# Down projection of a decoder layer: two chunk pairs as plain products, weight sums made in small units

## What is computed

```python
u, val = jnp.split(h2 @ p['w_up'], [D_FF], axis=-1)
u, fbuf_new = causal_dwconv(u, fbuf, p['ffconv_w'], p['ffconv_b'])
x = x + g2 * ((jax.nn.silu(u) * val) @ p['w_down'])      # (2048 + 32, 2816) @ (2816, 1024)
...
y_prompt = rms_norm(h_p, final_w)
```

## Time and profile before

| | us |
|---|---|
| median of 3 runs | 2711.03 (2708.97 to 2712.45) |
| profiled execution, device time | 2711.22 |
| its span on the trace | 2709.4 |
| end of the up stage, start of the down stage | 2240.4 |
| last matmul of the 88 steps ends | 2687.3 |
| TensorE busy, share of the span | 2463.4 (91%) |

### The profile page before, as it was taken

The page is one execution under the profiler, slowest core; times in us unless marked ns, Lnnn a source line. Parts: engine busy times, 40 slices in busy tenths (PEclk is TensorE's granted clock), DMA queues, the critical chain, the costliest instruction groups (busy, mean ns, idle before and its releaser), DMA issues. The chain is left out here.

```text
span 2709.4 us, 44409 instructions
## 1 busy us (share of the span) xinstructions
PE 2463.4 (91%) x17038; PEld 1519.8 (56%) x17038; DVE 1884.9 (70%) x3863; ACT 913.0 (34%) x1376; POOL 403.2 (15%) x384
## 2 busy tenths in 40 slices
PE   3899999879889999599969999999999986899997
PEld 1455555567677777455546666666666652344443
DVE  4555556446888887578866777777777779867666
ACT  1433433214444445144422222222222224322222
POOL 0132322300000000012332221222122200000000
PEclk6899999989999999599989999999999997899999
DMA  7434443460242312233312221122212214333323
GB/s 259 153 103 142 162 143 107 148 195 21 86 172 95 124 58 63 88 121 120 120 51 74 74 78 62 62 73 78 74 49 73 79 63 164 117 90 105 105 87 93
DMA packets 197350, 279.80 MB, mean 103 GB/s; under 512 B 19023, under 2 KB 134271, under 8 KB 195059
## 3 DMA queue, kind: packets, MB, share of 16 engines
q1 hardware_dynamic: 196965, 278.18, 31.4%
q10 hardware_dynamic: 270, 0.10, 0.0%
HBM read 202.95 MB, written 75.29 MB: 103 GB/s over the span
## 5 line engine op out<-in xcount | busy, mean ns | idle before, releaser
L2553 PE MATMUL py<-h_parts,w_heads 128*128 128x384 f16 (+1 forms) x792 | 246.0, 311 | 19.1 <-DVE u_p L2710 19.1
L2554 PE MATMUL py<-h_parts,w_heads 128*128 128x384 f16 (+1 forms) x792 | 245.8, 310 | 0.0
L2555 PE MATMUL py<-h_parts,w_heads 128*128 128x384 f16 (+1 forms) x792 | 245.8, 310 | 0.0
L336 PE MATMUL prj<-w_heads,h_parts_t 128*128 128x512 f16 x512 | 196.1, 383 | 12.3 <-PEq L451 6.2
L337 PE MATMUL prj<-w_heads,h_parts_t 128*128 128x512 f16 x512 | 195.8, 382 | 0.0
L338 PE MATMUL prj<-w_heads,h_parts_t 128*128 128x512 f16 x512 | 195.7, 382 | 0.0
L336 PE MATMUL m_prj<-m_h,w_heads 128*128 128x128 f16 (+1 forms) x1088 | 179.7, 218 | 11.6 <-DMA m_h<-h_parts 10.3
L2553 PE MATMUL px<-h_parts,w_heads 128*128 128x384 f16 (+1 forms) x528 | 164.4, 311 | 17.5 <-PEq L1884 17.5
L337 PE MATMUL m_prj<-m_h,w_heads 128*128 128x128 f16 (+1 forms) x1088 | 179.6, 218 | 0.0
L338 PE MATMUL m_prj<-m_h,w_heads 128*128 128x128 f16 (+1 forms) x1088 | 179.6, 218 | 0.0
L336 PE MATMUL d_pm<-d_w,w_heads 128*128 128x512 f16 x392 | 153.3, 391 | 24.4 <-DVE w_heads L2416 24.4
(11 more groups left out here) (550 smaller groups left out, 6017.1 us busy)
## 6 DMA issues: line engine op xcount, KB each, us to landing
C_new<-in_w_up_dram SPq DMA_DIRECT2D x11, 2048.0 KB, 7.5
w_heads<-in_w_up_dram SPq DMA_DIRECT2D x44, 512.0 KB
d_a<-act_cols SPq DMA_DIRECT2D x174, 128.0 KB, 2.2
act_cols<-w_heads SPq DMA_DIRECT2D x44, 384.0 KB, 2.3
win_raw<-in_w_ada_dram SPq DMA_DIRECT2D x8, 2048.0 KB
first_a<-in_w_down_dram SPq DMA_DIRECT2D x22, 512.0 KB
wa<-in_w_ada_dram SPq DMA_DIRECT2D x4, 2048.0 KB, 11.5
x_t<-in_x_prompt_dram SPq DMA_DIRECT2D x16, 512.0 KB, 4.1
```

What stands on the lines that cost most here:

```text
L336: nc.tensor.matmul(out, left[0], right[0], start=(k == 0), stop=False)
L2553: nc.tensor.matmul(out, left[0], right[0], start=(start and k == 0), stop=False, skip_group_check=True)
L2554: nc.tensor.matmul(out, left[0], right[1], start=False, stop=False, skip_group_check=True)
L2555: last = nc.tensor.matmul(out, left[1], right[0], start=False, stop=(k == KC // 2 - 1), skip_group_check=True)
```

## The change

The first two pairs (`PLAIN = 2`, steps 0 to 21) are multiplied as 8 plain products, 24 matmuls per step, two accumulating into one of 4 banks per pair (`plain_step`, `OF_PLAIN`); both pairs have banks of their own, 8 together. They need only four weight operands: three own blocks and one difference (`turn_w`, made in place in the raw block), cut by one instruction each (`hi_own`, `lo_own`, 2048 elements per partition), and six activation operands (four blocks and two sums that one instruction makes). The results of the plain pairs go straight from PSUM through the gate (`plain_scale`).

The three other weight sums, which the Winograd form needs from step 22 on, are made in 22 units of 256 columns, one per step from step 8 on: unit u's raw blocks are loaded again into one buffer (`load_unit`, two transfers of 256 KB), summed on VectorE at step u + 8 (`sums_unit`, three instructions), cut high on ScalarE in the same step (`hi_unit`), cut low on VectorE in the next (`lo_unit`). The loop bodies, shortened:

```diff
@@ DownParts
+    PLAIN = 2
+    UNITS, UNIT_AT = 2 * J, 8
+    OF_PLAIN = (((0, 1), (1, 3)), ((4, 2), (0, 0)), ((2, 1), (3, 3)), ((5, 2), (2, 0)))
...
+    def turn_w(self, dve, j):
+        b = self.raw(j)
+        self.w_landed(dve, j)
+        self.nc.vector.tensor_tensor(b[:, 0], b[:, 0], b[:, 2], ALU.subtract).then_inc(self.w_turned, 1)
...
+    def load_unit(self, sp, u):
+        if u:
+            sp.wait_ge(self.t_summed, u)
...
+        for h in range(2):
+            sp.dma_start(self.unit_raw()[:, 2 * h:2 * h + 2], src[:, h]).then_inc(self.unit_in, 16)
+    def sums_unit(self, dve, u):
+        q, t = self.unit_raw(), self.tsum
+        dve.wait_ge(self.unit_in, 32 * u + 32)
+        dve.wait_ge(self.t_lo, u)
...
+    def hi_unit(self, act, u):
+        act.wait_ge(self.t_summed, u + 1)
...
+    def lo_unit(self, dve, u):
+        dve.wait_ge(self.t_hi, u + 1)
...
@@ SyncE
             for n in range(1, J):
                 dn.load_a(sp, n)
                 if n + 1 < J:
                     dn.load_w(sp, n + 1)
+                unit_for(n)                     # load_unit(n - 9)
@@ ScalarE
             for j in range(1, J):
...
                 dn.hi_own(act, j)
-                dn.hi_sums(act, j)
                 dn.cut_a_hi(act, j)
+                unit_hi(j)                      # hi_unit(j - 8)
             for n in range(J, N):
                 dn.cut_a_hi(act, n)
-                if j == 0:
+                if j == 0 and i > dn.PLAIN:
                     keep(i - 1)
+                unit_hi(n)
                 if j == 3:
                     square(2 * i - 2)
@@ VectorE
             for j in range(1, J):
-                dn.lo_part(dve, j, 0)
                 if j + 1 < J:
-                    dn.sums_w(dve, j + 1)
-                dn.lo_part(dve, j, 1)
+                    dn.turn_w(dve, j + 1)
+                dn.lo_own(dve, j)
                 dn.sums_a(dve, j + 1)
                 dn.cut_a_lo(dve, j)
+                unit_work(j)                    # lo_unit(j - 9), sums_unit(j - 8)
...
+                if j == 0 and i == dn.PLAIN:
+                    plain_scale(2 * i - 2)
+                    plain_scale(2 * i - 1)
...
+                unit_work(n)
+                if n == J + 2:
+                    dve.wait_ge(s["const"], 32)
+                    plain_scale(0)
+                    plain_scale(1)
                 if j == 2:
                     residual(2 * i - 2)
@@ phase_up, last block of columns
-                    if g == 2 and last:
-                        dn.hi_sums(act, 0)
...
-                            dn.sums_w(dve, 0)
                             dn.sums_a(dve, 0)
...
-                            dn.lo_part(dve, 0, 0)
+                            dn.lo_own(dve, 0)
...
+                    if last and g == 0:
+                        dn.turn_w(dve, 0)
...
-            dn.lo_part(dve, 0, 1)
             dn.cut_a_lo(dve, 0)
```

More of the change, by code:

```diff
@@ new lines, in lo_own, with unit, unit_raw @@
+    def lo_own(self, dve, j):
+        dve.wait_ge(self.w_hi, j + 1)
+        w = self.slot(j)
+        self.nc.vector.scalar_tensor_tensor(out=w[:, 1, 0:4], in0=self.raw(j), scalar=self.core.mscale[:, 1:2], in1=w[:, 0, 0:4],
+                                            op0=ALU.mult, op1=ALU.subtract).then_inc(self.w_lo, 1)
+    def unit(self, n):
+        return n - self.UNIT_AT if 0 <= n - self.UNIT_AT < self.UNITS else None
+    def unit_raw(self):
+        return self.first[:, 0:D].rearrange("p (q n) -> p q n", q=4)
@@ L2387, in load_a, with plain @@
             sp.dma_start(raw[:, c], src[c]).then_inc(sem, 16)
+    def plain(self, n):
+        return n < self.PLAIN * self.J
     def sums_a(self, dve, n):
@@ L2947, in save, with unit_for @@
                 sp.dma_start(dst, out_of(k)[0:rows(k)]).then_inc(s["saved"], 16)
+            def unit_for(n):
+                u = dn.unit(n - 1)
+                if u is not None:
+                    dn.load_unit(sp, u)
             for n in range(1, J):
@@ L2983, in bank_free, with plain_step @@
             def bank_free(m, i):
-                if m in (0, 4):
-                    pe.wait_ge(s["kept"], 2 * i + 1 + (m == 4))
-                else:
-                    pe.wait_ge(s["folded"], 5 * i + 1 + (5, 1, 6, 3, 2).index(m))
+                if i < dn.PLAIN:
+                    pe.wait_ge(s["emptied"], {0: 2, 1: 4, 2: 4, 3: 4, 5: 5, 6: 6, 4: 7}[m])
+                elif m in (0, 4):
+                    pe.wait_ge(s["kept"], 2 * (i - dn.PLAIN) + 1 + (m == 4))
+                else:
+                    pe.wait_ge(s["folded"], 5 * (i - dn.PLAIN) + 1 + (5, 1, 6, 3, 2).index(m))
+            def plain_step(n):
+                i, j = divmod(n, J)
+                pe.wait_ge(dn.a_lo, n + 1)
+                pe.wait_ge(dn.w_lo, j + 1)
+                a, w = dn.a_parts(n), dn.slot(j)
+                for bank, pair in zip(banks[i], dn.OF_PLAIN):
+                    for t, (x, y) in enumerate(pair):
+                        last = three_passes(nc, bank, [a[:, p, x] for p in range(2)], [w[:, p, y] for p in range(2)], j or t, j == J - 1 and t == 1)
+                    if j == J - 1:
+                        last.then_inc(dn.prod, 1)
+                if j < J - 1:
+                    last.then_inc(dn.k_done, 1)
             def step(n):
@@ L3019, in _ @@
                     tops.spread_rows(pe, 2)
-                step(n)
+                if dn.plain(n):
+                    plain_step(n)
+                else:
+                    step(n)
             decode()
@@ L3124, in _, with unit_work @@
             nc.vector.memset(half[:], -0.5).then_inc(s["half"], 1)
-            dn.sums_w(dve, 1)
+            dn.turn_w(dve, 1)
             dn.sums_a(dve, 1)
+            def unit_work(n):
+                done, u = dn.unit(n - 1), dn.unit(n)
+                if done is not None:
+                    dn.lo_unit(dve, done)
+                if u is not None:
+                    dn.sums_unit(dve, u)
             for j in range(1, J):
-                dn.lo_part(dve, j, 0)
                 if j + 1 < J:
-                    dn.sums_w(dve, j + 1)
-                dn.lo_part(dve, j, 1)
+                    dn.turn_w(dve, j + 1)
+                dn.lo_own(dve, j)
                 dn.sums_a(dve, j + 1)
                 dn.cut_a_lo(dve, j)
+                unit_work(j)
                 if j == 2:
```

152 lines of the change are left out of this document (78 added, 74 removed).

## The result

The changed kernel takes 2732.10 us (median of 4 runs, 2730.92 to 2732.65), the kernel before, beside it on the same chip, 2710.33 (2708.97 to 2712.45): a ratio of 1.0082 (95% interval 1.0070 to 1.0095), 21.8 us slower. The forecast was 2719.2, slower by 8.0; the sign and the range (2707 to 2735) held, the size did not. The profiled execution has a span of 2729.0 against 2709.4.

| | before | forecast | measured |
|---|---|---|---|
| step 1 | 13.9 | 11.2 | 11.05 |
| step 9 | 86.2 | 57.7 | 61.8 |
| step 10 | 93.3 | 66.5 | 70.7 |
| step 12 | 102.3 | 78.7 | 85.2 |
| step 22 | 147.6 | 139.2 | 150.7 |

What follows compares the result with a forecast made beforehand. VectorE was taken to bound pair 0 and TensorE everything from step 10; 2711.2 + (193.4 - 184.0) for step 30's later start - 1.4 for the stage's start gave 2719.2 us, range 2707 to 2735.

Steps and rivals of the forecast that it cites:

- The beat as summed: Main case: VectorE and ScalarE taking turns set the pace in steps 11 to 29; 2707 to 2726 us, chance 0.70.
- the third rival: The unit's own load sets the beat, 7.2 us a round; step 30 at 209, 2735 us; chance 0.12.
- The bound before, and where the change counts: VectorE bounds pair 0, TensorE alone from step 10; behind step 30 both kernels are the same.
- The stage's start: End of the up stage: VectorE would end 1.9 us earlier; taken as -1.4 us (0 to -2.3).
- Steps 0 to 8: Step 1 starts at 11.2, then TensorE leads with 5.17 us a step; step 7 starts at 43.0.
- The new wait at step 9: Unit 0's loads queue behind block 10's, which waits for `lo_own(8)`; landing 49.7, step 9 at 57.7, step 10 at 66.5.
- The beat: Steps 11 to 29: VectorE and ScalarE wait for each other, 5.16 us a round in plain steps, 5.4 in Winograd steps.
- What is added to it: Other work and loads on top of the rounds: +10.8 us in steps 11 to 21, +11.1 in steps 22 to 29.
- activations behind the tiles (step 12): Step 12's activations, queued behind three 512 KB tiles, land after 5.4 us instead of 2.3: +1.8.
- loads behind stores (steps 17, 20): In steps 11 to 21, loads queued behind the 512 KB stores add 1.0 us.
- The first rival: TensorE stays the bound and all unit work hides beside it; step 30 at 156.0, 2682 us; chance 0.14.
- The rule on small transfers: Skill's rule: transfers below 2 KB carry large overhead, putting a unit's half nearer 1 MB's 5.0 us than the activations' 2.3.

Runs made afterwards that it cites:

- the second buffer: Changed kernel with odd units' loads landing in a second buffer, so each is issued a step earlier: 2718.87 us; together with ScalarE's order 2696.83 us.
- ScalarE's order: Changed kernel with ScalarE making a unit's high cut one step later, behind the next activation cut: 2715.95 us, 1.0021 of the kernel before.

## Why the prediction was right, and where it was too small

- **The range held in part by luck.** The beat as summed, which had the chance of 0.70, ended at 2726 with its bounds, 6 us below the measurement. Up to 2735 the range reached only for the third rival, and that one's condition, a unit's sums that wait for their load in most steps, did not come (9 of the 21 steps 9 to 29).
- **The bound before, and where the change counts:** right. Nothing moved behind step 32. Two readings were loose: VectorE is busy 8.9 of 9 us in the second window of the earlier trace rows only (7.3 in the first), and the earlier trace rows has three of the nine pauses, beside step 0's.
- **The stage's start**, -1.4: the profiled execution has -2.5. Ten kernels that are alike up to there start between 2236.0 and 2238.9, 1.7 to 4.5 us ahead of the one trace of before (2240.56). So the term was too small; by how much, one trace of before does not tell.
- **Steps 0 to 8**, `lo_own(8)` done at 43.2: it came at 46.1. Step 1 started as forecast (11.05), but the first eight matmuls behind its pause of 3.73 us ran at the lower level, 3.32 us in place of 8 x 0.2155 = 1.72, 1.6 lost, which stood only in the upper bound; the two small products of the maxima in step 3 took 0.4; and `lo_own(8)` ended 1.0 us behind step 7's start, not 0.2.
- **The new wait at step 9:** right in mechanism. Unit 0 landed 7.7 us after block 10's issue, not 6.5, and the row of work behind it took 7.9, as summed (8.0). Step 10 followed after 8.9 (8.8).
- **The beat:** 5.22 and 5.46 us, where 5.16 and 5.4 were summed.
- **What is added to it.** By low cuts, steps 12 to 22, over 5.15 each, in us:

| term | forecast | measured |
|---|---|---|
| activations behind the tiles (step 12) | 1.8 | 4.2 |
| four scales and a residual (step 14) | 2.4 | 2.7 |
| two norms (steps 15, 18) | 2.8 each | 2.7, 2.6 |
| loads behind stores (steps 17, 20) | 1.0 | 2.9 + 2.0 |
| the rest | 0 | 0.8 |
| sum | 10.8 | 18.0 |

The terms of instructions are right to 0.3 us, the terms of transfers too small by a factor of two to five. In steps 23 to 30, over 5.4 each, it is 12.2 instead of 11.1, and again the scales (2.7 for 3.0) and norms (3.2 for 3.4) fit and the residuals' loads (2.8 for 1.3) don't. The step that came out too small is how these were sized: as a transfer queued behind other bytes, with nothing added for a late issue. What was left out is that the queue stands: SyncE waits for a unit's sums, and behind that wait lie the tiles, the next activations, the stores and the residual rows. With the second buffer, which takes the standing away, and without unit loads, which takes the units' transfers away, these terms come to 0.1 and 0.9 us at step 12 instead of 4.2, to 0.1 and 0.2 at steps 17 and 20 together instead of 4.9, and to 0.5 for the residuals instead of 2.8: it takes both, the standing and the transfers, to make them. Of the 11.6 us by which the forecast was short (spans, 19.6 against 8.0), 4.1 stand at step 9 (2.9 of them from steps 1 to 8 and 1.2 from the landing), 7.2 in steps 11 to 21, 1.1 in steps 22 to 29, and about 1 went back at the stage's start.

- **The first rival**, 2682 with TensorE as the bound: the run without units has 2682.28, but by two differences that cancel. Up to pair 2's copy it gains 25.0 us, where 28.0 were summed, and the stage starts 4.3 earlier, where 1.4 was taken. Its condition was wrong: it was to decide "as soon as `hi_unit` doesn't hold up the next activation cut". With that done the kernel was at 2715.95, and the unit's single buffer still cost 18.2 us of the stage (201.6 against 183.4 with the second buffer).
- **The third rival**, the unit's load as the beat: priced at 7.2 us a round, it is 5.6 (sums 1.35, issue and landing 4.2). The beat of turns is so near to it that VectorE waited for a unit's landing nine times, eight of them for 0.2 to 1.6 us, and that each limit hid the other.
- **The rule on small transfers.** Half a unit, 256 KB in runs of 1 KB, lands in 3.3 us (median of 42 in steps 9 to 29), nearer to the activations' 2.3 than to the 5.0 of 1 MB, as the row had it; the activations in the same stretch take 3.2. The Trainium skill (Perfetto Trace Analysis, DMA Optimizations) says that small transfers carry a large overhead each; read as a rule on runs, as the prediction read it, it put the half unit nearer to the 1 MB row, and this trace does not agree. SyncE's own time does not go by bytes alone: two loads of half a unit keep it for 1.20 us, two of activations for 0.88 or more, one of 1 MB for 0.37.

## What to carry to other kernels

A step that two in-order engines hand back and forth costs the sum of both their works per round, however idle each looks; moving one instruction behind the next round's leading one undoes that, but look first for the second limit that is nearly as long, here a single-buffered load. A wait on a DMA-issuing queue is to be priced with all that stands behind it, not only with the transfer it belongs to. Instructions can be summed from rows, to 0.3 us here; what transfers add was two to five times the sum, so give it a wide bound.

## What was not expected of the hardware

TensorE's clock did not go by the length of a pause alone, and the first matmul behind a pause does not tell what follows. In the changed kernel the matmuls behind pauses of 2.43 us (step 18), 2.61 (step 28) and 3.40 (step 23) ran at the lower level from the first on (0.61). Behind 3.96 us at step 12 and 2.50 at step 15 the first was still short (0.39), but the level fell within the step, at the fourth matmul and at the second:

```profile
2323.87 0.52 PE L336 MATMUL d_pm<-d_w,w_heads 128*128 128x512 f16 x1
2324.19 0.63 PE L337 MATMUL d_pm<-d_w,w_heads 128*128 128x512 f16 x1
```

Nine matmuls of step 12 and eight of step 15 follow each other at up to 0.43 us, and each of these steps takes 6.88 us in place of 5.17. Behind 2.33 us at step 29 none is slow. With the second buffer a pause of only 2.00 (step 10) cost eight such matmuls, while with ScalarE's order pauses of 2.52, 2.78 and 2.83 (steps 12, 14 and 20) cost none; what decides between them was not tested. Within the beat it cost nothing: the next low cut came 5.22 us on behind step 10, with no slow matmul, and as much behind steps 12, 15 and 18, with seven to nine. Where TensorE leads, as in step 1, it cost the 1.6 us.
